# Moving steps between stages of a two-block transformer kernel: gate order, state stages, a fence, and the head of the recurrence

## The chip, the cores and the metric

The kernel runs on one core of a Trainium2 chip, as one program with an instruction stream for each engine: TensorE (PE) for matrix products, VectorE (DVE), ScalarE (ACT) and GpSimd (POOL) for the rest, and SyncE (SP), which issues most DMA transfers. ACT issues some transfers too, from its own stream. Every engine runs its instructions in program order and waits on semaphores for the others. The metric is the device time of one execution in microseconds, lower is better; the time of a version is the median of its runs.

## The reference

Two blocks follow each other on a sequence of 512 rows of width 1024, all in fp32. The first has three branches on an input normed and modulated by a condition: a state-space scan in four groups and both directions, a windowed attention that also looks at a context of 256 rows, and gates that merge them; then a feed-forward with a convolution. Cut to what the change touches:

```python
mod = jax.nn.silu(c) @ w_mod[l] + b_mod[l]                      # also for the context
h_lat = modulate(x, norm1_g[l], sh1, sc1)                       # rmsnorm(x, g) * (1 + sc1) + sh1
p_lat = h_lat @ w_in                                            # z, xbc, dt, q, k, v, gates
xbc = jax.nn.silu(dwconv_centred(xbc_raw, conv_w, conv_b))
states = jnp.einsum('bcsgn,bgrcs,bcsgrp->bcgrpn', bc, decay_to_end, xc)   # per chunk of 128
att_lat = window_ctx_attention(q_l, k_l, v_l, k_c, v_c, sink)
out = (g_ssd * (y_ssd @ w_o_ssd) + g_att * (y_att @ w_o_att)) @ w_out
```

The second block has a forgetting attention, a complex diagonal recurrence (s5) and an attention on a memory:

```python
log_f = jax.nn.log_sigmoid(fl + b_forget)                       # softplus, 12 heads
F = jnp.cumsum(log_f, axis=1)                                   # added to the scores of y_fox
ab = exp(lam * step); bb = (ab - 1) / lam * b                   # numbers of the recurrence, complex
x_re = jnp.einsum('gph,blgh->blgp', bb_re, u)
h = associative_scan(ab, x)                                     # along the 512 rows
y = Re(c h) + d * u
```

## The kernel before

**Products.** A product in fp32 is made as three products of halves: every operand is split into a high part (a cast to fp32r) and a low part (the rest), and PE adds high x high, low x high and high x low (L792 to L794, or L849 to L851 with the roles changed). So a projection of 128 output columns for 512 rows takes 24 matmuls of 128x512 over the eight parts of its input. Weights arrive in blocks of 512 KB. SP issues them (L2658) in a fixed order into four slots of raw weights (`raww`, RAWS = 4). ACT casts the high part (`whi`, L1243), POOL subtracts for the low part (`wlo`, L2486). A slot is free for the block four places later when its subtraction is done; a block of `w_mod` isn't split, PE reads it raw (L928), and its slot is free after that. ACT's casts stand in its stream among its other work, two split blocks ahead of PE (AHEAD = 2). What else ACT does at that place has to wait until the block has landed.

**Order.** `order()` writes one list of steps, and every engine runs its share of each step in that order. Lists of two tasks are merged by `merge()`, which takes the next step from the task that is behind by the costs in SHARE; `alternate()` takes them in turn. The steps that matter here:

- `mod j n`: a quarter of modulation row j, PE L928. `modt` and `modsel` (L936) bring a row into columns, `modout` writes shift `modS` and, for the scale, `A1` (L1933).
- `rms in`: the inverse root of the mean squares, spread over the partitions in PSUM by PE (L831). `xnorm j` multiplies `xin` by it (L1921). `h1 j` makes hv = xin·A1 + modS (DVE L1945 and L1946, for j = 1, 4, 7 on ACT), its high part `hT_h` on ACT (L1262) and its low part `hT_l` on DVE (L1707) for even j, POOL (L2502) for odd j. `dtx` multiplies two parts of h by the first weights, dt and one xbc block, which `bring` loads and splits.
- `dt 0` to `dt 5`: softplus of dt, its running sums, their transposes `csT`, which ACT writes to DRAM (`csd`, L1338 and L1342) for later loads of `ec`. `taps g m`: a convolution of B or C (`BTs`, ACT L1271, DVE L1755 and L1758).
- `state g d n`: in each of four groups, ten steps of xw = xtok·wdec on DVE (L1803), its product with B on PE (L1018) and the update of the state. They are merged in groups 1 to 3 with four projections `z` (gated by ACT and DVE into `yg`, ACT L1396 to L1404) and eight quarters of modulation rows. The `ssd_chunks` behind them are merged with the next group's xbc projections.
- `fence att`, `reload`, `qpair k`: the attention's output qT becomes the pair `qp_h`, `qp_l` for the projection `oa`; reload brings `yp` back from DRAM (L1478). The 16 projections `gate` stand beside the window attention.
- In the second block: `u` (the s5 input), `fl` and `forget` (PE L808, DVE L2367, softplus L1763 to L1776 with ACT L1266 and L1268, scan L2374), `s5num` (the numbers of the recurrence, in `pk`, DVE L1823, ACT L1534 to L1538), `s5bar`, 22 steps `s5pow` of powers, `fq`/`tm` (q, k and v of the attention), and `fscore`, `fpt`, `fpv` (scores L1182, row maximum L1781, exponential `Pf` L1278).

## Time and profile before

| | us |
|---|---|
| median of 3 runs | 2195.9 |
| lowest and highest run | 2193.11 and 2197.08 |
| the profiled execution | 2190.85 |
| its span | 2188.4 |

| engine | busy us | share of the span |
|---|---|---|
| PE (matmuls) | 2031.3 | 93% |
| DVE | 1068.3 | 49% |
| ACT | 863.1 | 39% |
| POOL | 815.3 | 37% |

The span is the time between the first and the last instruction of the profiled execution; what lies around it is 2.45 us. The trace is read as timelines: the instructions of an engine with their start, their duration and, in brackets, the time for which the engine stood idle before and what ended that. "x2" at the end of a row means that two instructions that follow each other are one row. Rows of ACTq and SPq are the time in which an engine's queue issues transfers, not the transfer. The granted clock is the share of full speed that PE was given.

### The profile page before, as it was taken

How to read it: one execution, taken by the hardware profiler on the slowest of the kernel's cores; microseconds unless marked ns; L12 is line 12 of the kernel's file. 1: busy time of each engine (PE TensorE's matmuls, PEld its weight loads, DVE VectorE, ACT ScalarE, POOL GpSimd, SP SyncE). 2: the span in 40 equal slices, each digit the busy share in tenths (PEclk: the TensorE clock that was granted, in tenths of full speed). 3: DMA queues.
4: the chain of work that ended last, by engine and by line, in shares of the span. 5: the costliest groups of instructions: out<-in, count | busy, mean ns of one | idle time of the engine just before them, and what ended most of it. 6: DMA issues, size and time to landing. Idle time of an engine off the chain costs nothing.

```text
span 2188.4 us, 28557 instructions
## 1 busy us (share of the span) xinstructions
PE 2031.3 (93%) x11586; PEld 1648.7 (75%) x11586; DVE 1068.3 (49%) x1741; ACT 863.1 (39%) x1563; POOL 815.3 (37%) x455
## 2 busy tenths in 40 slices
PE   4879898999999999999899999988898988999997
PEld 3758686878877787888778888876677766788886
DVE  4469685858455545531444441137544565611112
ACT  2435353535344444323343443233544443532221
POOL 1302121212343323466443444442532461544442
PEclk8999999999999999999999999989999999999998
DMA  7234545354211114323244333334112323243331
GB/s 261 68 110 155 183 144 195 134 177 160 87 58 39 49 41 162 116 95 109 87 135 135 97 94 96 99 108 135 58 58 63 86 55 86 81 134 97 96 106 58
DMA packets 89251, 235.63 MB, mean 108 GB/s; under 512 B 27424, under 2 KB 30624, under 8 KB 88224
## 3 DMA queue, kind: packets, MB, share of 16 engines
q1 hardware_dynamic: 85712, 225.16, 31.8%
q10 hardware_dynamic: 3408, 8.65, 1.0%
q8 instruction: 91, 1.49, 0.3%
q14 instruction: 40, 0.33, 0.0%
HBM read 220.51 MB, written 12.19 MB: 106 GB/s over the span
## 4 chain that ended last, share of the span: by engine, by line
PE 80%; DVE 12%; ACT 4%; issue 1%; DMA 1%; POOL 1%; SPq 0%; ACTq 0%; DVEq 0%; POOLq 0%
PE ps L792 21%; PE ps L794 20%; PE ps L793 20%; PE ps L1123 1%; PE ps L1018 1%; PE ps L1110 1%; PE ps L1182 1%; PE ps L1098 1%; PE ps L928 1%; PE ps L1040 1%; DVE ec L2052 1%; PE ps L1038 1%; PE ps L1039 1%; DVE xw L1803 1%; PE ps L1099 1%
## 5 line engine op out<-in xcount | busy, mean ns | idle before, releaser
L2486 POOL TENSOR_TENSOR wlo<-raww,whi 128x1024 fp32r<-128x1024 f32 (+2 forms) x253 | 590.0, 2338 | 949.5 <-ACT whi L1243 945.2
L1243 ACT CAST whi<-raww 128x1024 fp32r<-128x1024 f32 (+2 forms) x284 | 285.1, 1007 | 251.5 <-PE ps L794 183.8
L792 PE MATMUL ps<-hT_h,whi 128*128 128x512 f32 (+1 forms) x688 | 260.6, 379 | 7.4 <-DVE BTs L1758 6.8
L794 PE MATMUL ps<-hT_h,wlo 128*128 128x512 f32 (+1 forms) x688 | 251.9, 366 | 0.0
L793 PE MATMUL ps<-hT_l,whi 128*128 128x512 f32 (+1 forms) x688 | 251.8, 366 | 0.0
L792 PE MATMUL ps<-H_h,whi 128*128 128x512 f32 x480 | 190.6, 397 | 9.7 <-ACT qk L1554 4.1
L793 PE MATMUL ps<-H_l,whi 128*128 128x512 f32 x480 | 187.3, 390 | 0.0
L794 PE MATMUL ps<-H_h,wlo 128*128 128x512 f32 x480 | 187.1, 390 | 0.0
L792 PEld LDWEIGHTS ps<-hT_h,whi 128*128 128x128 f32 x688 | 131.1, 191 | 32.7 <-DVE BTs L1758 7.1
L1796 DVE SCALAR_TENSOR_TENSOR gt<-gt,ps 128x512 f32<-128x512 f32 x40 | 27.5, 688 | 250.8 <-PE ps L794 250.8
L793 PEld LDWEIGHTS ps<-hT_l,whi 128*128 128x128 f32 x688 | 131.0, 190 | 22.5 <-issue 2.6
L794 PEld LDWEIGHTS ps<-hT_h,wlo 128*128 128x128 f32 x688 | 130.5, 190 | 21.2
L792 PE MATMUL ps<-h_h,whi 128*128 128x512 f32 x336 | 132.2, 393 | 0.8 <-ACT mk L1526 0.8
L793 PE MATMUL ps<-h_l,whi 128*128 128x512 f32 x336 | 131.1, 390 | 0.0
L794 PE MATMUL ps<-h_h,wlo 128*128 128x512 f32 x336 | 130.9, 389 | 0.0
L792 PEld LDWEIGHTS ps<-H_h,whi 128*128 128x128 f32 x480 | 90.5, 189 | 33.4 <-ACT qk L1554 5.5
L794 PEld LDWEIGHTS ps<-H_h,wlo 128*128 128x128 f32 x480 | 90.2, 188 | 19.2
L793 PEld LDWEIGHTS ps<-H_l,whi 128*128 128x128 f32 x480 | 90.3, 188 | 18.6 <-issue 0.5
L1389 ACT ACTIVATE ec<-ec,la 128x128 f32<-128x128 f32 x256 | 77.3, 389 | 52.9 <-DVE ec L2052 52.9
L1755 DVE SCALAR_TENSOR_TENSOR ua<-ps,vc,ua 128x511 f32<-128x511 f32 x44 | 33.0, 750 | 109.7 <-ACT ua L1271 109.7
L1781 DVE TENSOR_REDUCE small<-ps 128x1 f32<-128x513 f32 (+1 forms) x64 | 48.3, 755 | 72.5 <-PE ps L1103 52.9
L792 PEld LDWEIGHTS ps<-h_h,whi 128*128 128x128 f32 x336 | 63.1, 188 | 15.8 <-issue 1.6
(521 smaller groups left out, 4676.1 us busy)
## 6 DMA issues: line engine op xcount, KB each, us to landing
ec<-csd SPq DMA_DIRECT2D x32, 1024.0 KB, 7.8
raww<-in_w_mod SPq DMA_DIRECT2D x48, 512.0 KB, 4.7
raww<-in_w_up SPq DMA_DIRECT2D x44, 512.0 KB, 3.7
raww<-in_w_xbc SPq DMA_DIRECT2D x24, 512.0 KB, 4.5
raww<-in_w_gl SPq DMA_DIRECT2D x24, 512.0 KB, 3.4
raww<-in_w_z SPq DMA_DIRECT2D x16, 512.0 KB, 4.8
raww<-in_w_g SPq DMA_DIRECT2D x16, 512.0 KB, 3.4
raww<-in_w_os SPq DMA_DIRECT2D x16, 512.0 KB, 3.7
```

Source lines behind the costliest of these rows:

```text
L792: e.matmul(o, whi[:, i, c], hi(k)[:, t0:t1], start=(k == 0), stop=False)
L793: e.matmul(o, whi[:, i, c], lo(k)[:, t0:t1], start=False, stop=False)
L794: last = e.matmul(o, wlo[:, i, c], hi(k)[:, t0:t1], start=False, stop=(k == kt - 1))
L928: last = e.matmul(ps[32 * q:32 * q + 32, b, 0:128], cs_[:, 4 * n + 2 * kk:4 * n + 2 * kk + 32], raww[:, p % RAWS, kk * 512 + q * 128:kk * ...
L1018: e.matmul(ps[:, b, :], Btok[:, CHUNKS[d][n], :], xw[:, i, :], start=True, stop=True).then_inc(*ssd_done.mark(("state", g, d, n), ("free", ...
L1038: e.matmul(o, xtok[:, c, h], inner(g, c, 0)[:, r, :], start=True, stop=False)
L1243: e.copy(o, x.rearrange("p (k c) -> p k c", c=64) if p == plan.first["dt", 0] else x).then_inc(*w_high.mark(("high", p)))
L1389: last = e.activation(E[:, r, :], E[:, r, :], ACT.Exp, bias=la[:, c, h:h + 1])
L1755: e.scalar_tensor_tensor(out=dst[:, 1:T], in0=psum[:, 0:T - 1], scalar=V(names[0], m), in1=dst[:, 1:T], op0=ALU.mult, op1=ALU.add).then_in ...
L1781: e.tensor_reduce(sm[:, 1:2], S, AXX, ALU.max, negate=True).then_inc(*v_step.mark(event))
L1796: e.scalar_tensor_tensor(out=x, in0=x, scalar=1.0, in1=psum, op0=ALU.add, op1=ALU.mult).then_inc(*v_moved.mark(*events))
L2486: e.tensor_tensor(o, x, h.bitcast(F32), ALU.subtract).then_inc(*p_wlow.mark(("split", p), ("raw free", p)))
```

## The change

- **Start.** `bring` goes ahead of all of `w_mod`. `xnorm` is gone: DVE makes hv = xin·A1·(spread root) from PSUM in one scalar_tensor_tensor for each of the two widths (512 and 256), ACT adds the shift while it writes the high part, and DVE makes the low part, (hv + modS) - hT_h, in two pieces, for all eight rows. POOL has no part in it any more. The spread root lies in PSUM until the last row is made, so that the ring of banks for `rms in` is one shorter. `dtx 0` stands behind the last quarter of row 3.
- **SHARE.** New costs. They move `taps(0,4)` ahead of `dt 5`, and small steps elsewhere.
- **State stages 1 to 3.** `z_mod_steps` writes the order of z projections and modulation quarters by hand, in place of `alternate`.
- **Fence att.** PE doesn't wait there for the other engines; `gate 15` stands behind the fence, ahead of the pairs; `reload` comes after `gateout 15` and waits for that projection.
- **Second block.** `fl` and `forget` stand ahead of `u 4`, `u 5`, the first `fq` and `s5num`. Of the 22 `s5pow` steps 16 stood ahead of the first `fscore` and 6 behind it; now 6 stand ahead and 16 behind.

```diff
-SHARE = {"dt": 2.4, "x1": 1.2, "state0": 10.56, "xbc0": 5.76, "xbc1": 13.1, "taps0": 0.05, "taps1": 0.01,
+SHARE = {"dt": 2.4, "x1": 1.92, "state0": 6.34, "xbc0": 5.18, "xbc1": 13.1, "taps0": 0.36, "taps1": 0.01,
...
+def z_mod_steps(g, j, k):
+
+    z, m = z_steps(g), lambda j: [(SHARE["mod"], [("mod", j, n)]) for n in range(4)]
+    a, b, t = m(j), m(k), lambda j: [(0.1, [("modt", j)])]
+    sel = lambda j: [(0.1, [("modsel", j)]), (0.0, [("modout", j)])]
+    return (z[:1] + a[:2] + z[1:3] + a[2:] + t(j) + z[3:6] + sel(j) + b[:2] + z[6:9] + b[2:] + t(k) + z[9:11] + sel(k) + z[11:])
...
-    return out + sum((gate_steps(i) for i in range(11, 16)), [])
+    return out + sum((gate_steps(i) for i in range(11, 15)), [])
...
-    o = [("init",), ("norm1",)] + a[0] + a[1] + a[2] + [("total", "in")] + a[3] + [("modt", 0)]
...
-    o += c[3] + [("modt", 1), ("h1", 2), ("xnorm", 4), ("bring",), ("h1", 3), ("xnorm", 5)]
-    o += d[0] + [("modsel", 1), ("modout", 1)] + d[1] + [("xnorm", 6), ("dtx", 0)] + d[2] + [("xnorm", 7)] + d[3] + [("modt", 3), ("dtx", 1)]
-    o += [("modsel", 3), ("modout", 3), ("h1", 4), ("h1", 5), ("dtx", 2), ("h1", 6), ("h1", 7), ("dtx", 3)]
+    o = [("init",), ("norm1",), ("bring",)] + a[0] + a[1] + a[2] + [("total", "in")] + a[3] + [("modt", 0)]
...
+    o += d[0] + [("modsel", 1), ("modout", 1)] + d[1] + [("h1", 3)] + d[2] + d[3] + [("modt", 3), ("dtx", 0), ("modsel", 3), ("modout", 3)]
+    o += [("h1", 4), ("dtx", 1), ("h1", 5), ("h1", 6), ("dtx", 2), ("h1", 7), ("dtx", 3)]
...
-    o += merge(ssd_states(1), alternate(z_steps(0), mod_steps((4, 5)))) + merge(ssd_chunks(1), xbc_steps(2))
...
+    o += merge(ssd_states(1), z_mod_steps(0, 4, 5)) + merge(ssd_chunks(1), xbc_steps(2))
...
-    o += [("fence", "att"), ("reload",)] + [("qpair", k) for k in range(8)]
+    o += [("fence", "att"), ("gate", 15)] + [("qpair", k) for k in range(8)] + [("gateout", 15), ("reload",)]
...
-    o += [("fence", "two"), ("s5load",), ("s5num",), ("u", 4), ("u", 5)] + [("s5u", m) for m in range(3)]
-    chain = [(SHARE["fl"], [("fl",)]), (SHARE["forget"], [("forget",)]), (SHARE["fq"], [("fq", 0)]), (SHARE["fq"], [("fqout", 0), ("fq", 6)]), (0.0, [("fqout", 6)])]
+    o += [("fence", "two"), ("fl",), ("s5load",), ("forget",), ("u", 4), ("u", 5), ("fq", 0), ("s5num",)] + [("s5u", m) for m in range(3)]
+    chain = [(SHARE["fq"], [("fqout", 0), ("fq", 6)]), (0.0, [("fqout", 6)])]
...
                     elif s[1] == "att":
                         fence(PE, "att")
-                        others(PE, "att")
...
+                    ACTE.wait_ge(at("h", j))
+                    ACTE.wait_ge(at("mod", j))
+                    v = hv[:, j % 4, :]
+                    e.activation(hT_h[:, j, 0:L], v[:, 0:L], ACT.Identity, bias=modS[:, j, 0:1]).then_inc(*x_high.mark(("high part", "hT", j)))
+                    e.activation(hT_h[:, j, L:LT], v[:, L:LT], ACT.Identity, bias=modS[:, j, 1:2]).then_inc(*x_high.mark(("high part", "hT", j)))
...
+            def shifted_low1(j):
+                DVE.wait_ge(at("high part", "hT", j))
+                DVE.wait_ge(at("mod", j))
+                for q, (t0, t1) in enumerate(ALL):
+                    last = e.scalar_tensor_tensor(out=hT_l[:, j, t0:t1], in0=hv[:, j % 4, t0:t1], scalar=modS[:, j, q:q + 1],
+                                                  in1=hT_h[:, j, t0:t1].bitcast(F32), op0=ALU.add, op1=ALU.subtract)
...
+                    for q, (t0, t1) in enumerate(ALL):
+                        last = e.scalar_tensor_tensor(out=v[:, t0:t1], in0=xin[:, j, t0:t1], scalar=A1[:, j, q:q + 1], in1=r[:, t0:t1], op0=ALU.mult, op1=ALU.mult)
...
+                    if j:
+                        shifted_low1(j - 1)
```

How the order shows on the engines, at three places. First ACT around dt 5, before and after; `csd` is DRAM, `BTs_78` the B of group 0, `wdec` and `csT` come from dt's sums:

```order
53 L1334 ACTIVATE wdec<-wdec 128x384
54 L1243 CAST whi<-raww 128x1024
55 L1338 DMA csd<-csT 2x32x128 x4
56 L1339 ACTIVATE ecsT<-csT 64x512
57 L1342 DMA csd<-ecsT 2x32x128 x4
58 L1271 ACTIVATE BTs_78<-ps,vc 128x512
59 L1271 ACTIVATE BTs_78<-ps,vc 128x256
```

```order
56 L1327 ACTIVATE wdec<-wdec 128x384
57 L1240 CAST whi<-raww 128x1024
58 L1268 ACTIVATE BTs_78<-ps,vc 128x512
59 L1268 ACTIVATE BTs_78<-ps,vc 128x256
60 L1331 DMA csd<-csT 2x32x128 x4
61 L1332 ACTIVATE ecsT<-csT 64x512
62 L1335 DMA csd<-ecsT 2x32x128 x4
63 L1357 ACTIVATE sq<-BTs_78 128x512
```

The two activations into BTs_78 now stand ahead of the eight issues into csd.

Second, the end of state stage 1 on PE, before and after, from the last products of the last z projection (L794, in the new file L792) to the step that turns the modulation row. The raw modulation blocks are `raww`, the state products `xw,Btok`:

```order
830 L794 MATMUL ps<-hT_h,wlo 128x512
831 L928 MATMUL ps<-raww,cs__56 32x128 x8
832 L1018 MATMUL ps<-xw,Btok 128x512
833 L928 MATMUL ps<-raww,cs__56 32x128 x8
834 L1018 MATMUL ps<-xw,Btok 128x512
835 L928 MATMUL ps<-raww,cs__56 32x128 x8
836 L1018 MATMUL ps<-xw,Btok 128x512
837 L928 MATMUL ps<-raww,cs__56 32x128 x8
838 L1018 MATMUL ps<-xw,Btok 128x512
839 L936 MATMUL ps<-cst,mrow 128x8
```

```order
830 L792 MATMUL ps<-hT_h,wlo 128x512
831 L926 MATMUL ps<-raww,cs__56 32x128 x8
832 L1016 MATMUL ps<-xw,Btok 128x512
833 L926 MATMUL ps<-raww,cs__56 32x128 x8
834 L1016 MATMUL ps<-xw,Btok 128x512
835 L934 MATMUL ps<-cst,mrow 128x8
```

Behind the last z projection stood four modulation blocks, each with a state product; now two do, and the other two stand ahead of its 24 matmuls.

Third, the head of the recurrence on DVE, before and after. `ffs` are the forget gates, `FT` their sums, `apow` and `pk` the recurrence's powers and numbers, `X` the residual rows:

```order
1003 L1823 TENSOR_TENSOR apow<-apow,vtmp 128x24x2
1004 L1763 SCALAR_TENSOR_TENSOR ffs<-ffs 12x512
1005 L1765 TENSOR_SCALAR ffs<-ffs 12x512
1006 L1767 SCALAR_TENSOR_TENSOR ffs<-ffs 12x512
1007 L1770 RECIPROCAL ffs<-ffs 12x512
1008 L1772 SCALAR_TENSOR_TENSOR ffs<-ffs 12x512
1009 L1774 TENSOR_TENSOR ffs<-ffs 12x512
1010 L1776 SCALAR_TENSOR_TENSOR ffs<-ffs 12x512
1011 L2374 SCALAR_TENSOR_TENSOR FT<-cst,ffs 12x512
```

```order
975 L2236 SCALAR_TENSOR_TENSOR X<-X,vc,ps 128x512 x8
976 L2367 TENSOR_SCALAR ffs<-ps,vc 12x512
977 L1767 SCALAR_TENSOR_TENSOR ffs<-ffs 12x512
978 L1769 TENSOR_SCALAR ffs<-ffs 12x512
979 L1771 SCALAR_TENSOR_TENSOR ffs<-ffs 12x512
980 L1774 RECIPROCAL ffs<-ffs 12x512
981 L1776 SCALAR_TENSOR_TENSOR ffs<-ffs 12x512
982 L1778 TENSOR_TENSOR ffs<-ffs 12x512
983 L1780 SCALAR_TENSOR_TENSOR ffs<-ffs 12x512
984 L2374 SCALAR_TENSOR_TENSOR FT<-cst,ffs 12x512
985 L2249 MEMSET Tp 128x1024
986 L1827 TENSOR_TENSOR pk__63<-vc,pk__63 128x24 x2
```

The gates' softplus and scan stood behind the numbers and the first powers; now they follow the last rows of X, and the numbers come behind them.

## Rows read from the trace of the kernel before

**Rows 1.** The page, part 1: busy us (share of the span) xinstructions.

```profile
PE 2031.3 (93%) x11586; PEld 1648.7 (75%) x11586; DVE 1068.3 (49%) x1741; ACT 863.1 (39%) x1563; POOL 815.3 (37%) x455
```

**Rows 2.** Windows: us, busy us (instructions) by engine, granted clock, DMA share, GB/s.

```profile
250.00:275.00 25.00, 19.50 (x128) 13.48 (x127) 22.63 (x29) 11.39 (x26) 5.05 (x3) 0.86 0.50 162
...
845.00:870.00 25.00, 20.08 (x111) 15.47 (x111) 14.93 (x17) 11.46 (x20) 11.63 (x7) 0.86 0.68 269
1490.00:1550.00 60.00, 46.24 (x234) 36.71 (x232) 49.52 (x143) 20.85 (x38) 18.00 (x8) 0.86 0.28 86
```

**Rows 3.** Timeline of PE at the start: start, us, engine, line, operation [idle <-releaser].

```profile
40.60 1.08 PE L928 MATMUL ps<-raww,cs__56 128*32 128x128 f32 x16 [4.20 <-DMA raww<-in_w_mod]
...
47.16 0.80 PE L959 MATMUL ps<-hT_h,whi 128*128 128x512 f32 x1 [3.94 <-DVE xin L1921]
...
61.13 0.79 PE L959 MATMUL ps<-hT_h,whi 128*128 128x512 f32 x1 [3.73 <-DVE hT_l L1707]
```

**Rows 4.** Timeline of SP at the start; then source L2186 (ns min/median/max).

```profile
31.80 0.40 SPq L2658 DMA_DIRECT2D raww<-in_w_dt  x1
...
L2186 DVE SCALAR_TENSOR_TENSOR vt<-X,A,ps x8: 742/748/748, 1060.8 to 1078.2; 128x512 f32<-128x512 f32 x8
```

**Rows 5.** Timelines of ACT and its queue, then PE, at dt 5.

```profile
117.09 2.68 ACTq L1338 DMA_DIRECT2D csd<-csT  x4
...
122.63 1.23 ACT L1271 ACTIVATE BTs<-ps,vc 128x512 f32<-128x512 f32 x2 [2.19 <-issue]
...
125.03 0.80 PE L792 MATMUL ps<-hT_h,whi 128*128 128x512 f32 x1 [6.83 <-DVE BTs L1758]
```

**Rows 6.** Timelines in state stage 1: PE, SP, ACT, DVE, POOL; last, tile xw's DVE line.

```profile
256.57 1.12 PE L1018 MATMUL ps<-xw,Btok 128*128 128x512 f32 x2
...
263.77 2.05 PE L1018 MATMUL ps<-xw,Btok 128*128 128x512 f32 x2 [5.50 <-DVE xw L1803]
...
253.44 9.99 SPq L2658 DMA_DIRECT2D raww<-in_w_xbc  x6
...
256.84 1.05 ACT L1243 CAST whi<-raww 128x1024 fp32r<-128x1024 f32 x1 [6.45 <-DMA raww<-in_w_xbc]
...
260.79 2.83 DVE L1803 TENSOR_TENSOR xw<-xtok,wdec 128x512 f32<-128x512 f32 x1
...
260.68 2.40 POOL L2486 TENSOR_TENSOR wlo<-raww,whi 128x1024 fp32r<-128x1024 f32 x1 [0.36 <-ACT whi L1243]
...
L1803 DVE TENSOR_TENSOR xw<-xtok,wdec x40: 680/685/2839, 130.0 to 493.6; 128x512 f32<-128x512 f32 x40
```

**Rows 7.** Timelines at the fence "att": ACT and its queue, then PE.

```profile
853.75 1.91 ACTq L1478 DMA_DIRECT2D yp_l<-ysc  x4
855.69 4.26 ACT L1262 CAST qp_h<-qT 128x512 fp32r<-128x512 f32 x8 [4.44 <-issue]
...
857.89 0.77 PE L792 MATMUL ps<-qp_h,whi 128*128 128x512 f32 x1 [4.92 <-ACT qp_h L1262]
...
861.44 0.63 PE L794 MATMUL ps<-qp_h,wlo 128*128 128x512 f32 x1
...
864.10 0.39 PE L793 MATMUL ps<-qp_l,whi 128*128 128x512 f32 x1
864.33 0.39 PE L794 MATMUL ps<-qp_h,wlo 128*128 128x512 f32 x1
```

**Rows 8.** Timelines at the start of the s5 stage: ACT, DVE, then PE.

```profile
1504.66 0.63 ACT L1266 ACTIVATE ffs<-ffs 12x512 f32<-12x512 f32 x1 [14.22 <-DVE ffs L1763]
...
1516.97 1.21 DVE L2374 TENSOR_TENSOR_SCAN FT<-cst,ffs 12x512 f32<-12x512 f32 x1
...
1513.04 0.55 PE L849 MATMUL ps<-whi,H_h 128*128 128x256 f32 x1 [6.91 <-POOL wlo L2486]
...
1539.04 1.65 PE L1182 MATMUL ps<-qk 128*128 128x384 f32 x2 [4.32 <-ACT Pf L1278]
...
1549.97 0.91 PE L1182 MATMUL ps<-qk 128*128 128x384 f32 x2 [0.24 <-ACT Pf L1278]
```

More of the change, by code:

```diff
@@ L1053, in tensor_program @@
                     if n == "in":
[L1054 removed]
+                        spread(("rms", n), 3, LT, (5,), at("root", n))
                     elif n == "x2":
@@ L1476, in scalar_program @@
                 elif k == "reload":
+                    ACTE.wait_ge(at("gemm", ("gate", 15), 0))
                     for i in range(4):
@@ L1725, in shifted_low @@
                                        op0=ALU.add, op1=ALU.subtract).then_inc(*v_xlow.mark(("pair", "h2", j), ("free", "vt2", j)))
+            def shifted_low1(j):
[4 more added lines that the diff above has]
+                                                  in1=hT_h[:, j, t0:t1].bitcast(F32), op0=ALU.add, op1=ALU.subtract)
+                    if q == 0:
+                        last.then_inc(*v_xlow.mark(("pair", "hT", j)))
+                last.then_inc(*v_xlow.mark(("pair", "hT", j), ("free", "hv", j)))
             def rms(n):
```

72 lines of the change are left out of this document (22 added, 50 removed).

## The prediction

> **What bounds the kernel now.** I read the page's list of busy times first: TensorE (PE) is busy for 93% of the span, 2031.3 us, and the other engines for half or less [rows 1]. So about 157 us is all that a new order can win in idle time, beside what the clock gives back. The second view is the table of stretches, where a reader should see that PE's idle time isn't even. In three short stretches PE is busy for 19.50 of 25, 20.08 of 25 and 46.24 of 60 us, and the granted clock is 0.86 there [rows 2]. The third view is the timeline of PE with what ended each idle time, and then the same stretch on the engine named. Each hole is followed by slow work: the pair of state products that takes 1.12 us ahead of the hole that ends at 263.77 takes 2.05 us after it [rows 6], the ratio of the 2.4 to the 1.2 GHz level. A hole costs its idle time, and some 2 to 3 us of slower products behind it.
>
> **The change part by part.** All terms are made against the profiled execution, 2190.85 us (span 2188.4); the median of the runs, 2195.9, is 5.05 above it, and I carry the difference over. No arithmetic of weight on PE is added or removed: the change moves steps in all five engines' programs.
>
> *Start (h1).* PE waits 4.20 us for a block of w_mod, 3.94 for `xin` from VectorE (DVE) and 3.73 for `hT_l` [rows 3]. Removed are eight products of 128x768 on DVE, the two-step tensor_scalar of five of the rows there and that of three on ScalarE (ACT), and the low parts of four rows on GpSimd (POOL). Added, for each of the eight rows, are a product from PSUM of 512 columns, which takes 0.748 in the norm of the second half of the block [rows 4], one of 256 (estimate 0.45), and the low part in two pieces (0.7 and 0.45, from the same width). That is some 2.4 us for each row on DVE, 19 in all, which is no less than what goes. It isn't a gain in itself. What gains is the order. The weights of dt and the first xbc block are now loaded ahead of w_mod, not at 31.80 behind twelve of its blocks [rows 4], and dtx 0 stands behind the last mod rather than amid them. Against it, w_mod's third and later blocks wait until ACT and POOL have split the two blocks in front, which I put at 4.6 us from casts and subtractions that take 1.05 and 2.40 each elsewhere [rows 6], partly beside each other. Of 3.94 + 3.73 + 4.20 = 11.9 us of waits and some 3 us of clock, less 4.6 and less about 5 us in which DVE paces the last four rows (4 x 2.4, half of it beside PE's work), there remain 5.5 us. The bounds are 0 (DVE paces all) and 9.
>
> *dt 5 and the taps.* PE stands still for 6.83 us until `BTs` are there. ACT had not come to them: it issued four transfers of csd from 117.09 for 2.68 us and four more after that, and began with BTs at 122.63 [rows 5]. The issues alone hold ACT back by 5.5 us. In the new order taps(0,4) stands ahead of dt 5, so BTs starts at about 117 and the issues run while DVE and PE work. The price is the delay of csd, whose reader, the load of ec, isn't due before the chunks. Gain: the 6.83, less some 3 that ACT and DVE need for BTs in any order (from 122.63 to 125.03 and a little more), plus 2 of clock, is 6; bounds 3 and 9.
>
> *State stages 1 to 3.* In stage 1 PE finishes the last mod block at about 258.3 and waits 5.50 us for `xw`; the two later stages have the same hole (one of three is shown). Followed back: DVE's xw takes 2.83 us beside a subtraction of 2.40 on POOL, against a median of 0.685 over 40; DVE had itself waited for ACT's sq, and ACT had waited 6.45 us for the first block of w_xbc, which SyncE (SP) could issue only at 253.44, when PE had freed a slot of raw weights [rows 6]. In the old order four mod blocks stand behind the last z product; in the new one two stand ahead of it and two behind, so the slot of the first xbc block comes free before z's 24 products of 0.23 us from start to start [rows 7], 5.5 us earlier. ACT's cast then lies behind PE's work, its sq is not late, and xw is not late either. Each hole is worth 5.5 plus 2.6 of clock. I take 6 (18 for three), since ACT, DVE and POOL still have the same work in the same few microseconds. Bounds: 10 and 24.
>
> Here the Trainium skill bears on the row, in "SBUF — State Buffer", section "SBUF: two separate sides": VectorE with two operands in SBUF and GpSimd reading SBUF hold a shared pair of ports as "an exclusive lock, not a bandwidth split". The 2.83 beside POOL's 2.40 agrees. By this rule the hole would shrink only as far as POOL's subtraction moves off xw: if it still meets xw, 2.1 us remain in each stage and the three give 12, not 18.
>
> *The fence "att".* PE waits 4.92 us until `qp_h` is there, because ACT issues four transfers (1.91 us) before its casts and PE has nothing in between [rows 7]. Now one projection of 24 products (gate 15, 5.5 us) stands there, and the transfers are issued after it. It covers the wait whole; with the 15 or so products behind it that took 0.63 rather than 0.39 each (3 us, since they overlap) the hole is worth 7.9. Left over is what gate 15 lost where it stood, as cover for the last window softmax. Gain 6.5; bounds 3 and 7.5.
>
> *Start of the recurrence (s5).* The forget gates end with a scan at 1516.97. ACT had waited 14.22 us for DVE with their first exponential, and all its casts of weights stood behind that. PE therefore waited 6.91 us at 1513.04 for wlo, and 4.32 at 1539.04 for `Pf`, where the row maximum stood behind DVE's power steps [rows 8]. The stretch lacks 60 - 46.24 = 13.8 us of PE and 14% of its clock [rows 2]. In the new order forget stands ahead of the numbers and the first power steps, so its scan ends at least those 14.22 us earlier, by 1504, and ACT's wait lies where DVE has nothing else to do and is short. Idle 13.8 and clock 4 are the most there is. I take 11: both waits (11.2), plus 3 of clock, less 3 for ten more power steps (16 rather than 6) among the scores. There they cost little so far: PE's wait at 1549.97, with a step on either side, is 0.24 [rows 8]. Bounds 5 and 17.
>
> *The rest.* Small moves in the window stage and the late s5 steps touch small waits like that 0.24 each: 0, bounds -5 and +5.
>
> **The sum** is 5.5 + 6 + 18 + 6.5 + 11 + 0 = 47 us: 2190.85 - 47 = 2143.9 profiled, 2195.9 - 47 = 2149 on the runs' scale.
>
> **Rivals.** *Holes move on* (a half gain). The xbc block comes earlier, but one resource later is as late: z's own block must now be loaded and split behind two mod blocks, and POOL's subtraction meets xw. The state stages then give 9, and in the s5 stage ACT's wait moves from softplus to the numbers' three activations, which gives 6 less; the start gives 0. Sum 9 less, 6 less and 5.5 less: 26, or 2170. For it speak the 2.83 of xw; against it, that ACT's wait of 6.45 names a transfer, not POOL.
>
> *All holes close* with the clock: each bound's upper part, 5.5 + 8 + 23 + 7.5 + 15 = 59, or 2137. It needs DVE off the path everywhere.
>
> *The power steps land on the scores* (slower). Sixteen steps stand among scores whose row maximum queues behind them on DVE. If each is stretched by POOL as xw is, by 2.1 us, and its own length, an estimate of 1.4 us from the steps' small operations, is exposed as well, that is 16 x 3.5 = 56, less the 47: 9 us slower, 2205. It decides from 47 / 16 = 2.9 us exposed for each step. The wait of 0.24 beside such a step speaks against it.
>
> *Nothing gained*: the waits swap places and the times stay, 2196. It would need every term at its low bound and the last at its worst (0 + 3 + 10 + 3 + 5 - 5 = 16, still faster), so it is unlikely.
>
> **How the numbers follow.** The forecast, 2141 to 2160, has a chance of 0.50; all holes closing 0.15; holes moving on 0.27; nothing gained 0.03; slower 0.05. Faster by over 0.2% (4.4 us, about what a measurement of this kernel can tell from no change) is 0.92, within it 0.03, slower 0.05. The range runs from the sum of all upper bounds, 9 + 9 + 24 + 7.5 + 17 = 66.5, which is 2129, and 1 for the runs' spread, to 2170 and 6 more for the last term's bound and the same spread: 2128 to 2176.
>
> **What would show it.** Right: no PE wait above 2 us behind the last mod block in the three state stages; ACT's BTs ahead of csd and PE's wait there under 2 us; gate 15 between the last window product and the first with qp_h, and no wait; the scan ended by 1504 and the second score block of the forgetting attention reached 10 us earlier than 1539; no PE wait of over 3 us between dtx 1 and dtx 3. Wrong: a PE wait on a z product's `wlo` in a state stage, xw at 2.8 again with PE waiting, ACT idle behind `pk` with casts queued, or PE waiting for Pf by over 1 us in several places of 1525 to 1590.

## The result and the profile after

The changed kernel takes 2174.36 us (median of 4 runs, 2171.24 to 2177.91) against 2195.87 before (2193.11 to 2197.08): the ratio is 0.9904, with a 95% interval of 0.9885 to 0.9923. It is 21.5 us faster where 47 were forecast. The profiled execution after took 2175.76 us (span 2174.4), against 2190.85 before; it gained 15.1 us, less than the medians, since it lies 1.4 us above the median of its kernel and that of before 5.0 below. Of the runs below one (stages 2 and 3 undone) took 4804.77 us, where the four others of its kernel took 2171 to 2180, and is left out of its median.

The page's first part after, to be read beside [rows 1]: PE's instructions are as many, and what changed is above all its idle time. The span is 14.0 us shorter; 11.2 of that are idle time, and 2.8 are products that ran faster (mean granted clock 0.979, before 0.973).

```profile
PE 2028.5 (93%) x11586; PEld 1648.7 (76%) x11586; DVE 1075.7 (49%) x1749; ACT 863.2 (40%) x1565; POOL 813.3 (37%) x453
```

The windows after that hold the work of [rows 2] (us, busy us and instructions by engine, granted clock, DMA share, GB/s), and with them those of stages 2 and 3:

```profile
245.00:270.00 25.00, 24.43 (x162) 19.94 (x162) 23.24 (x29) 13.73 (x31) 9.06 (x4) 1.00 0.45 146
345.00:370.00 25.00, 21.20 (x134) 14.59 (x133) 20.17 (x28) 9.48 (x15) 7.45 (x3) 0.93 0.53 180
480.00:505.00 25.00, 20.04 (x173) 19.69 (x172) 20.77 (x25) 13.05 (x39) 2.45 (x1) 0.86 0.48 165
```

Stage 1 is full at full clock (24.43 of 25 us; 19.50 before). Stage 3's window isn't: there the hole is still 5 us and the clock 0.86.

**Where the time went.** Steps have moved, so a row of before has no row of after at its place. I therefore added up PE's rows of each trace in order of time, a product of n columns counted as n/512 x 0.2275 us (what one takes from start to start at full clock), and compared the times at which both kernels had the same amount of work behind them. I call this the ledger. The unit is such a microsecond of work; "gain" is how much further ahead the changed kernel got in that stretch. The fence's hole lies at 658.5, so the window stage is counted to 655.

| stretch (work done, us) | forecast | gain after |
|---|---|---|
| start, to the first dt products (0 to 40) | 5.5 | 1.4 |
| dt 5, taps and group 0 (40 to 160) | 6 | 8.2 |
| state stage 1 (160 to 200) | 6 | 6.3 |
| state stage 2 (200 to 300) | 6 | 0.9 |
| state stage 3 and its chunks (300 to 440) | 6 | -0.7 |
| window stage (440 to 655) | 0 | -8.8 |
| the fence "att" (655 to 680) | 6.5 | 7.0 |
| to the second block's last u (680 to 1260) | 0 | -0.4 |
| head of the recurrence (1260 to 1300) | 11 (whole stage) | 12.1 |
| the rest of that stage (1300 to 1520) | | -12.2 |
| to the end | 0 | 0.2 |
| sum | 47 | 14.0 |

One execution isn't the kernel. At the same order of steps, stage 1 gained 5.1 to 6.8 us in 16 traces (mean 5.9), stage 2 gained 0.9 to 5.2 in 15 (mean 3.0), and stage 3 with its chunks -2.2 to -0.6 in eight (mean -1.3). So the 0.9 of stage 2 in this trace is at the low end.

Three terms came as forecast (dt 5, stage 1, the fence, whose 6.5 was meant less what gate 15 costs the window stage), one was too large (the start), two gained next to nothing here (stages 2 and 3), the window stage lost what the fence won and more, and the head's gain was given back entirely. PE's rows with idle time say by what. Timeline of PE after:

```profile
364.32 1.33 PE L1016 MATMUL ps<-xw,Btok 128*128 128x512 f32 x2 [3.10 <-DVE xw L1807]
...
489.38 0.66 PE L1036 MATMUL ps<-ec,xtok 128*64 128x128 f32 x2 [4.96 <-DVE ec L2064]
...
605.91 0.33 PE L1107 MATMUL ps<-cst,Pm 128*128 128x128 f32 x1 [1.96 <-DVE Pm L1795]
...
729.71 0.65 PE L1120 MATMUL ps<-PT,vt 128*64 128x256 f32 x4 [2.24 <-DVE PT L2147]
...
845.16 0.47 PE L790 MATMUL ps<-qp_h,whi 128*128 128x512 f32 x1 [0.59 <-POOL qp_l L2502]
...
1559.09 1.65 PE L1179 MATMUL ps<-qk 128*128 128x384 f32 x2 [5.44 <-ACT Pf L1275]
...
1821.39 1.19 PE L1161 MATMUL ps<-Hp,Qc 128*128 128x128 f32 x4 [6.18 <-DMA Tp<-kd]
```

The 4.92 of [rows 7] is 0.59 at 845.16, the 6.91 of [rows 8] is 1.73 (at 1492.36), and the 6.83 of [rows 5] is gone. New are 4.96 us at 489.38 (for ec, in stage 3's first chunk; 1.11 before), 5.44 for Pf at 1559.09 and 6.18 for a transfer at 1821.39.

**Stage 1 against stage 2**, whose steps stand in the same order. Timelines of ACT, DVE and PE after; first stage 1, then stage 2:

```profile
242.93 1.05 ACT L1240 CAST whi<-raww 128x1024 fp32r<-128x1024 f32 x1 [6.29 <-DMA raww<-in_w_xbc]
...
247.55 2.85 DVE L1807 TENSOR_TENSOR xw<-xtok,wdec 128x512 f32<-128x512 f32 x1
...
250.54 1.10 PE L1016 MATMUL ps<-xw,Btok 128*128 128x512 f32 x2 [0.57 <-DVE xw L1807]
...
356.76 1.05 ACT L1240 CAST whi<-raww 128x1024 fp32r<-128x1024 f32 x1 [9.14 <-DMA raww<-in_w_xbc]
...
361.34 2.83 DVE L1807 TENSOR_TENSOR xw<-xtok,wdec 128x512 f32<-128x512 f32 x1
```

and the queue that issues the blocks, SP, in the same two places:

```profile
238.55 0.80 SPq L2654 DMA_DIRECT2D raww<-in_w_xbc  x2
...
350.73 9.24 SPq L2654 DMA_DIRECT2D raww<-in_w_xbc  x3
```

The block is 4.4 us under way in stage 1 (238.55 to 242.93) and 6.0 in stage 2 (350.73 to 356.76). From the issue to the end of xw it is 11.9 us and 13.4 us, and PE's cover (z's 24 products, two mod blocks, a state product) is some 11. So the hole is 0.57 in one and 3.10 in the other. Of the 2.5 us between them the landing makes 1.6; the other 0.9 is cover: PE reached the product 11.4 us after the issue in stage 1 and 10.5 in stage 2. Neither is a property of the stage. At this order the same block was under way for 3.8 to 5.6 us in stage 1 (16 traces) and for 3.8 to 6.0 in stage 2 (15), and the hole at the end of stage 2 was anything from under 0.5 us (three traces) to 3.1. In both, xw takes 2.85 and 2.83 us as before [rows 6]: POOL's subtraction still stands beside it.

### The profile page after: what moved, and what is told of

Read it like the earlier page. It is cut to its first block, busy times and chain, and to the rows that moved or that the text cites. A ratio compares the mean times of both kernels' runs of the same rounds, so it can differ in the third digit from the quotient of the medians.

```text
span 2174.4 us, 28587 instructions
## 1 busy us (share of the span) xinstructions
PE 2028.5 (93%) x11586; PEld 1648.7 (76%) x11586; DVE 1075.7 (49%) x1749; ACT 863.2 (40%) x1565; POOL 813.3 (37%) x453
## 3 DMA queue, kind: packets, MB, share of 16 engines
q1 hardware_dynamic: 85712, 225.16, 31.9%
## 4 chain that ended last, share of the span: by engine, by line
PE 80%; DVE 11%; ACT 4%; DMA 2%; issue 2%; POOL 1%; SPq 0%; ACTq 0%; DVEq 0%; POOLq 0%
PE ps L790 20%; PE ps L791 20%; PE ps L792 20%; PE ps L1107 1%; PE ps L1120 1%; PE ps L1095 1%; PE ps L1038 1%; PE ps L926 1%; PE ps L1179 1%; PE ps L1036 1%; PE ps L1016 1%; PE ps L1037 1%; PE ps L1039 1%; DVE xw L1807 1%; PE ps L1161 1%
## 5 line engine op out<-in xcount | busy, mean ns | idle before, releaser
L2486 POOL TENSOR_TENSOR wlo<-raww,whi 128x1024 fp32r<-128x1024 f32 (+3 forms) x255 | 596.5, 2345 | 980.3 <-ACT whi L1240 976.0
L792 PE MATMUL ps<-hT_h,wlo 128*128 128x512 f32 (+1 forms) x688 | 250.7, 364 | 0.0
L792 PE MATMUL ps<-H_h,wlo 128*128 128x512 f32 x480 | 187.0, 390 | 0.0
L792 PEld LDWEIGHTS ps<-hT_h,wlo 128*128 128x128 f32 x688 | 129.9, 189 | 21.0
L792 PE MATMUL ps<-h_h,wlo 128*128 128x512 f32 x336 | 130.8, 389 | 0.0
L792 PEld LDWEIGHTS ps<-H_h,wlo 128*128 128x128 f32 x480 | 90.1, 188 | 19.0
L1275 ACT ACTIVATE Pm<-ps,small 128x513 f32<-128x513 f32 (+1 forms) x64 | 47.6, 744 | 82.7 <-DVE small L1785 82.4
```

Source lines behind the costliest of these rows:

```text
L792: last = e.matmul(o, wlo[:, i, c], hi(k)[:, t0:t1], start=False, stop=(k == kt - 1))
L1275: e.activation(dst, S, ACT.Exp, bias=sm[:, 1:2], accum_out=sm[:, 2:3]).then_inc(*a_func.mark(event, drained))
L2486: e.tensor_tensor(o, x, h.bitcast(F32), ALU.subtract).then_inc(*p_wlow.mark(("split", p), ("raw free", p)))
```

## The experiments

The runs are given as medians, each beside the kernel before on the same chip, with the ratio and its interval. An interval is about 0.15 to 0.2% wide to each side, 3 to 4 us; so I also give the ledger of PE's work by stretch. In most stretches it repeats better: the window stage lost 8.6 to 9.9 us in six of the seven traces with the new order there and gate 15 behind the fence, and 5.4 in the seventh. A difference of 2 or 3 us that one trace shows in one stretch isn't shown by it alone.

**The window stage: order or missing gate?** Its loss of 8.8 us has two candidates in the diff: the new places of `q`, `qrot` and `gate`, or gate 15, which no longer covers the last rows.

```diff
-"score": 4.99, "pt": 1.4, "pv": 1.61, "q": 8.33, "qrot": 3.05, "kst": 0.84
+"score": 1.66, "pt": 1.12, "pv": 0.82, "q": 7.57, "qrot": 2.5, "kst": 0.0
-    return out + sum((gate_steps(i) for i in range(11, 15)), [])
+    return out + sum((gate_steps(i) for i in range(11, 15)), []) + [(SHARE["gate"], [])]
```

> The changed kernel, with the order of the window stage as before (without gate 15, which stays behind the fence). In the changed kernel PE does the work between the start of the window stage and the fence 9 us slower than before, by the work done against time. Theory: the new places of q, qrot and gate among scores cost this (PE waits for DVE's Pm and PT); then the window stage gets back 5 to 9 us, and the run is 5 to 9 us below the changed kernel (2166 to 2169). Rival: the loss is gate 15, which covered the last softmax rows and is missing there; then nothing comes back from the order and the run is within 2 us of the changed kernel (2174).

Measured: 2169.62 us, ratio 0.9885 (0.987 to 0.99). The window stage lost 2.0 us instead of 8.8, with gate 15 behind the fence as in the changed kernel, and the waits for Pm and PT there are those of before (1.05, 0.94 and 1.03 us). The seven later kernels with this order lost 2.0 to 2.1 us. The medians, 4.7 us apart, point the same way, but their intervals overlap.

```diff
-    return out + sum((gate_steps(i) for i in range(11, 15)), [])
+    return out + sum((gate_steps(i) for i in range(11, 16)), [])
-    o += [("fence", "att"), ("gate", 15)] + [("qpair", k) for k in range(8)] + [("gateout", 15), ("reload",)]
+    o += [("fence", "att"), ("reload",)] + [("qpair", k) for k in range(8)]
+                        others(PE, "att")
-                    ACTE.wait_ge(at("gemm", ("gate", 15), 0))
```

> The changed kernel, with the part at the fence undone: gate 15 among the window's steps, the reload ahead of the pairs, and PE's wait for all engines. Theory (order of q, qrot, gate is at fault in the window): the fence's 6.6 us hole comes back, the window loses as much as in the changed kernel, so 5 to 7 us slower than the changed kernel (2180). Rival (gate 15 is missed in the window): the window gets back what the fence loses, within 2 us of the changed kernel.

Measured: 2177.51, ratio 0.9926 (0.9908 to 0.9944), 3 us slower than the changed kernel, which the runs alone don't separate. By the ledger the stretch from 440 to 700 loses 5.6 us against 1.8 in the changed kernel: the fence's part is worth 3.8. With the window order of before that stretch gains 5.0, in all eight traces: 7.0 at the fence, less 2.0 for the cover that gate 15 gave in the window stage. So of the 8.8 us the order is at fault for 6.8 and the missing gate for 2.0: the new costs moved 5.5 us projections from ahead of DVE's row maxima to other places, where Pm and PT are waited for. (With the new order and the gate in its old place the window stage lost 5.5, not 8.8. Since one trace without the gate lost as little, a larger share of the gate at that order is neither shown nor excluded.)

**The second block: are the powers at fault for what is given back?** Both runs put the 22 power steps of the recurrence early again, by an empty step ahead of the other chain, the second with all costs of that block as before, which is exactly the order of before from the first q pair on.

```diff
-    chain = [(SHARE["fq"], [("fqout", 0), ("fq", 6)]), (0.0, [("fqout", 6)])]
+    chain = [(SHARE["fl"] + SHARE["forget"] + SHARE["fq"], []), (SHARE["fq"], [("fqout", 0), ("fq", 6)]), (0.0, [("fqout", 6)])]
```

> The changed kernel, with the 22 power steps of the recurrence placed early again, as far as an empty step ahead of the second chain does it (8 of them before the values of the attention, 16 before its first score), with the new costs otherwise. PE reaches the first score 23 us earlier than before and has given back 10 to 13 of that by 1830 us. Theory: the powers among the scores cost it (PE waits 5.44 us for Pf at 1559, beside power steps of DVE that take 1.0 us in place of 0.26); then 5 to 10 us come back (2164 to 2169). Rival: the gift is lost later anyway, since the recurrence's chain on DVE, POOL and DMA is the bound of that stage and only starts as early as its numbers allow; then within 2 us of the changed kernel.

> As the run with the powers early, and with the costs of all steps of the second block as before, which gives exactly the order of before from the first q pair on. If the new costs of the late s5 steps are at fault (the wait of 6.18 us for Tp from DRAM at 1821), this is 3 to 6 us faster than the run with the powers early alone; if the order isn't the reason, both are alike and as slow as the changed kernel.

Measured: 2208.34, ratio 1.006 (1.0041 to 1.0079), and 2175.75, ratio 0.9915 (0.9897 to 0.9933). Both theories fell for the first: it was 34 us slower than the changed kernel. The second is as fast as the changed kernel, 33 us faster than the first, where the theory had 3 to 6. They have 15 and 16 of the 22 powers ahead of the scores and differ in the costs alone. In both, PE's first wait for Pf is longer than it ever was (13.13 and 13.08 us), so this wait isn't what makes one of them slow; the ledger of 1300 to 1520 loses 33.8 us in the first and 3.4 in the second. Timeline of PE, powers early:

```profile
1524.04 1.65 PE L1179 MATMUL ps<-qk 128*128 128x384 f32 x2 [13.13 <-ACT Pf L1275]
```

**Three places outside the block** that the trace offered, with the window order of before: modulation row 3 is turned ahead of dtx 0, and in chunk 0 of group 3 another product of v covers ec.

```diff
-... + d[3] + [("modt", 3), ("dtx", 0), ("modsel", 3), ("modout", 3)]
+... + d[3] + [("modt", 3), ("modsel", 3), ("modout", 3), ("dtx", 0)]
+    late = [("tmout", "w_v", 0, 1), ("tm", "w_v", 0, 2)]
+    o = [s for s in o if s not in late]
+    i = o.index(("out", 3, 0))
+    o[i:i] = late
```

> The changed kernel with three edits in three stretches that don't touch: the window stage's order as before (as in the first run of this study); at the start the step that turns modulation row 3 ahead of dtx 0; in chunk 0 of group 3 the third product of v (tm, 2.9 us of PE) ahead of the outputs that wait for DVE's ec. Theory at the start: A1 of the last four rows waits on PE's order alone (the turn ran at 55.18 us, behind dtx 0), so DVE begins h1 4 some 6 us earlier and PE's waits of 2.10 and 1.58 go: 3 us. Theory in group 3: DVE's chain (xw, gating, ec) is what is late, and 2.9 of the 4.96 us can be covered: 3 us. Rival at the start: the load of the next blocks is late; at group 3: PE's extra step only moves the wait to the next chunk; then 0 each. Theory 2162 to 2165, rivals 2169.

Measured: 2162.06, ratio 0.9851 (0.9836 to 0.9866), as the theories had it. By the ledger the start gained 7.9 us against before (the four kernels with this start 5.8 to 7.9, mean 6.9; the nine without it -0.2 to 4.5, mean 2.5), and stage 3 with its chunks 3.9 instead of -0.7 (the seven kernels with this edit mean 3.1, the eight without it -1.3). PE's wait for ec (timeline of PE, three places) is 1.19, where it was 4.96:

```profile
480.78 0.40 PE L1033 MATMUL ps<-ec,xtok 128*64 128x128 f32 x2 [1.19 <-DVE ec L2061]
```

The turn that ran at 55.18 behind dtx 0 runs at 48.18, and the waits of 2.10 and 1.58 us between the dtx products are gone.

**POOL beside the powers.** In the changed kernel DVE and POOL meet where PE waits 5.44 us. Timelines of DVE, then POOL, after:

```profile
1550.00 1.00 DVE L1827 TENSOR_TENSOR q<-q,pk__63 128x96 f32<-128x96 f32 x1
1551.03 1.00 DVE L1827 TENSOR_TENSOR q<-q,vtmp 128x96 f32<-128x96 f32 x1
...
1549.81 1.08 POOL L2567 TENSOR_TENSOR BA<-bbar,arev 128x512 f32<-128x512 f32 x1
1550.85 1.07 POOL L2568 TENSOR_TENSOR ptmp<-bbar,arev 128x512 f32<-128x512 f32 x1
```

Each of these two operations of DVE lasts about as long as POOL's beside it; operations of the same shape took 0.26 us at 1546.74 and 1547.04, with POOL idle.

```diff
                     POOL.wait_ge(at("factor powers"))
+                    POOL.wait_ge(at("phase powers"))
```

> The changed kernel; POOL starts the first table of the recurrence only when DVE has made the last power (one wait more). In the changed kernel DVE's operations on q and pk took 1.00 and 2.47 us instead of 0.26 and 0.62 while POOL made that table at 1549.8 to 1556.9. Theory (POOL's collisions with the powers cause PE's wait of 5.44 us for Pf): that wait falls to 2 us or less and the run is 2 to 4 us faster. Rival (the time is set by the recurrence's chain, which now starts its table 7 us later): same or 1 to 3 us slower.

Measured: 2174.71, ratio 0.9913 (0.9901 to 0.9926). PE's wait at that place fell to 1.76 us, and the ledger, counted from the block's start, was 3.5 us better at 1340; at 1520 it was level. The collision is real and cost that wait; it isn't what the stage's end waits for. Timeline of PE, POOL behind the powers, at that wait:

```profile
1552.69 0.91 PE L1179 MATMUL ps<-qk 128*128 128x384 f32 x2 [1.76 <-ACT Pf L1275]
```

**Stages 2 and 3, and the second block, undone.** The first puts these two stages in exactly the order of before (the costs of before are set while they are merged; the chunks behind stage 3 keep their new places), the second the whole second block.

```diff
-    o += merge(ssd_states(2), z_mod_steps(1, 6, 7)) + merge(ssd_chunks(2), xbc_steps(3))
-    o += merge(ssd_states(3), z_mod_steps(2, 8, 9)) + merge(ssd_chunks(3), kv_steps())
+    o += with_costs_of_before(lambda: merge(ssd_states(2), alternate(z_steps(1), mod_steps((6, 7))))) + merge(ssd_chunks(2), xbc_steps(3))
+    o += with_costs_of_before(lambda: merge(ssd_states(3), alternate(z_steps(2), mod_steps((8, 9))))) + merge(ssd_chunks(3), kv_steps())
```

> The changed kernel, with state stages 2 and 3 in exactly the order of before; stage 1 keeps the new order. By the traces stage 1 gained 6 us and stages 2 and 3 together less than 1. Theory (DVE's work is the bound there, the holes moved inside the stage and into the first chunk): within 1.5 us of the changed kernel (2173 to 2176). Rival (the new order does gain in stages 2 and 3, and something else lost it): 6 to 12 us slower.

```diff
-    o += [("fence", "two"), ("fl",), ("s5load",), ("forget",), ("u", 4), ("u", 5), ("fq", 0), ("s5num",)] + [("s5u", m) for m in range(3)]
-    chain = [(SHARE["fq"], [("fqout", 0), ("fq", 6)]), (0.0, [("fqout", 6)])]
+    o += [("fence", "two"), ("s5load",), ("s5num",), ("u", 4), ("u", 5)] + [("s5u", m) for m in range(3)]
+    chain = [(SHARE["fl"], [("fl",)]), (SHARE["forget"], [("forget",)]), (SHARE["fq"], [("fq", 0)]), (SHARE["fq"], [("fqout", 0), ("fq", 6)]), (0.0, [("fqout", 6)])]
```

> The changed kernel, with the second block in exactly the order of before (gates behind the numbers, all costs of that block as before). PE reached the first scores 12.7 us earlier by the work done in the changed kernel and was no more ahead at 1860 us than at the block's start. Theory (the new order of that stage gains nothing in the end): within 2 us of the changed kernel. Rival (the forecast's: the head's gain is real and another thing lost it by chance in that trace): 8 to 12 us slower, 2182 to 2186.

Measured: 2175.53 (median of the four that count), ratio 0.9912 (0.9897 to 0.9927), and 2176.21, ratio 0.9919 (0.9905 to 0.9932). Neither differs from the changed kernel beyond the intervals. With the order of before, stage 2 gained 0.3 by the ledger (mean 3.0 with the new one) and stage 3 with its chunks 0.0 (-1.3): by these the new order of both is worth 1 to 2 us, and the medians, 1.2 us apart, don't speak against it. The new order of the second block is worth nothing measurable as a whole.

**What decides in the second block?** Four kernels on the one with three places (2162.06): costs of before with the new head; the same with 12 rather than 7 powers ahead of the scores; part of the powers' arithmetic left out; and the blocks brought later.

```diff
-"fv": 2.7, "fscore": 0.45, "fpv": 3.9, "s5bar": 3.3, "s5x": 4.0, "s5scan": 2.19, "s5tab": 8.71, "s5g": 4.62, "s5out": 6.33, "s5k": 1.02
+"fv": 3.0, "fscore": 0.36, "fpv": 3.12, "s5bar": 3.0, "s5x": 5.0, "s5scan": 2.43, "s5tab": 8.22, "s5g": 5.76, "s5out": 4.0, "s5k": 1.44
```

> The kernel with the three edits (2162), with all costs of the second block as before: the first score still has only 7 of 22 power steps ahead of it, the later steps of the recurrence stand up to one head later. Theory A (the total of DVE's work decides, the order of the late steps does little): within 3 us of 2162. Theory B (the new costs of the late steps are at fault for the 7 us lost between 1650 and 1720): 4 to 8 us faster.

```diff
+    chain = [(9.3, []), (SHARE["fq"], [("fqout", 0), ("fq", 6)]), (0.0, [("fqout", 6)])]
```

> As the run with the costs of before, with an empty step of half the cost ahead of the second chain: 12 of 22 power steps ahead of the first score. Theory A: each power step costs PE as much ahead of the scores as among them, so within 3 us of the run with 7 ahead. Rival: there is a place between where they lie beside PE's work; then 5 us or more faster than both.

```diff
-                        cmul((part(tab, 0, k, 2 * k), part(tab, 1, k, 2 * k)), (part(tab, 0, 0, k), part(tab, 1, 0, k)), (K(12), K(13)), k,
-                             vtmp[:, 0:24 * k].rearrange("p (a b) -> p a b", b=k))
+                        for q in (0, 1):
+                            tt(part(tab, q, k, 2 * k), part(tab, q, 0, k), K(12).unsqueeze(2).to_broadcast([P, 24, k]), ALU.mult)
```

> The kernel with the three edits (2162), leaving out part of the arithmetic of the powers: each of the six doublings of the tables z8 and q8 is two products instead of six operations on DVE, so that the recurrence's numbers are not the reference's. It takes 24 operations of 0.2 to 0.26 us plus their gaps, some 6 us, off DVE between 1500 and 1560 us. Theory (DVE's work decides the stretch up to the first scores and what is paid among them): 4 to 7 us faster, about 2157. Rival (another chain, of POOL or of transfers, decides at the end): the ledger of that stretch shows the gain and loses it by 1860 us, within 2 us of 2162.

```diff
-    o = [("init",), ("norm1",), ("bring",)] + a[0] + a[1] + a[2] + [("total", "in")] + a[3] + [("modt", 0)]
+    o = [("init",), ("norm1",)] + a[0] + a[1] + a[2] + [("total", "in")] + a[3] + [("modt", 0), ("bring",)]
```

> The kernel with the three edits (2162), with the blocks of dt and xbc brought after the fourth block of w_mod instead of ahead of the first. In the changed kernel the total of squares ran at 23.37 us (18.70 before), since PE stood in front of a w_mod block that came late, and all of h1 with it. Theory: the root is back at 27 us, the first row of h 5 us earlier, dtx 0 up to 4 us earlier: 2158 to 2160. Rival (PE's modulation blocks end late by the transfers whatever their order, at 49 us): within 1 us of 2162.

Measured: 2188.75 (0.9979, 0.9968 to 0.9989), 2186.23 (0.9963, 0.9948 to 0.9978), 2156.32 (0.9834, 0.9818 to 0.985) and 2158.8 (0.9845, 0.9829 to 0.9861). The first is 27 us slower, which neither theory had: A fell outright, and B had the wrong sign. The ledger loses 29 us between 1400 and 1520; PE's waits there are for Pq (11.9 us in all), Pf (7.4) and PTm (4.5). That the costs of before, with the powers late, put the late steps of the recurrence behind too much of the attention, where no projection is left to lay beside them, fits this, but isn't shown. Twelve power steps ahead don't help (second). Taking some 6 us of work off DVE gives 5.7 (third); the intervals of the two kernels just overlap, and the ledger of the block has 4.9. The medians don't tell the fourth from the kernel with three places, but by the ledger the start gains 2 to 3 us more with the blocks behind the fourth block of w_mod (8.5 to 10.8 in three kernels, mean 9.4, against 6.9).

In the ledger from 1260 to the end, the combinations stand like this: new costs with 6 powers ahead of the scores 1.0 to -4.4 (six traces), with 15 ahead -32.7 (two traces); costs of before with 7 ahead -31.9, with 12 ahead -26.7, with 16 ahead -2.4 and -2.0.

**The end of the stage, and the head alone.** The first two are edits on the fastest, 2158.8; the third is the changed kernel with the old head.

```diff
     o += merge(s5_steps(), chain)
+    o.remove(("gm", 3))
+    o.insert(o.index(("s5out", 5)), ("gm", 3))
```

> The fastest kernel so far (2158.8: three edits and bring later), with the projection gm 3 (5.5 us of PE) ahead of the recurrence's last output step instead of behind it. PE waited 6.05 us there for Tp, which comes back from DRAM. Theory (part of the head's gain is lost at this wait, since the other chain has nothing left to lay beside it): 3 to 5 us faster, 2154 to 2156. Rival (the projection was cover for the gelu behind that step, and its wait appears there): within 1.5 us of 2158.8.

```diff
                     POOL.wait_ge(at("factor powers"))
+                    POOL.wait_ge(at("phase powers"))
```

> As the run before, and POOL's first table waits for the last power. By the ledger of PE's work this wait alone saved 3 us at 1600 us and nothing at the stage's end. Theory (the stage's end was bound by the transfer then): now 2 to 3 us faster than the run before. Rival (the table comes late for the first g step in any case): same or slower.

> The changed kernel (2174) with the steps at the head of the recurrence in the order of before (numbers, then fl and forget) and all new costs kept. Theory A (DVE's work ahead of the scores is the bound, so the head's order is worth 2 us at most and the costs only fit themselves to it): 2174 to 2178. Theory B (head and costs belong together, as the slow run with the old costs says): 10 us slower or more, 2185.

Measured: 2162.33 (0.9865, 0.9849 to 0.9882), 2159.44 (0.984, 0.9827 to 0.9855) and 2206.53 (1.0057, 1.0044 to 1.0069). The wait for Tp is gone with gm 3 ahead of it, but nothing is gained: PE now waits 4.94 us there, at 1799.05, for a sq of DVE, as the rival had it. POOL's wait on top of that is 2.9 us faster by the medians, inside the intervals, and 0.5 by the ledger of the block.

The third run settles the head. Its steps from the first fq 6 on stand in exactly the order of the run with the powers early; only the head differs, and both take the same: 2206.53 and 2208.34. Their ledgers are 9 us apart at 1280 (the scan is early in one) and within 0.4 us of each other from 1300 to the end. The same holds with the order of before behind the head: 2175.75 with the new head, 2176.21 with the old, and -2.4 and -2.0 by the block's ledger. So at a fixed order of what follows, the head is worth nothing that the medians (2 us apart at most) or the ledgers (0.4 us) show, twice. Timelines of DVE: powers early, whose first row begins the forget gates and whose second is their scan:

```profile
1468.27 0.74 DVE L2367 TENSOR_SCALAR ffs<-ps,vc 12x512 f32<-12x512 f32 x1 [14.33 <-PE ps L808]
...
1480.10 1.21 DVE L2374 TENSOR_TENSOR_SCAN FT<-cst,ffs 12x512 f32<-12x512 f32 x1
```

and the head undone, numbers first:

```profile
1467.27 0.91 DVE L2249 MEMSET Tp<- 128x1024 f32 x1 [13.23 <-DMA xsc<-X]
...
1502.29 1.21 DVE L2374 TENSOR_TENSOR_SCAN FT<-cst,ffs 12x512 f32<-12x512 f32 x1
```

Timeline of PE, head undone, the first wait for Pf:

```profile
1524.30 1.65 PE L1179 MATMUL ps<-qk 128*128 128x384 f32 x2 [4.03 <-ACT Pf L1275]
```

The scan comes 22 us earlier with the new head, and the score behind it starts at the same time, 1524.04 against 1524.30. DVE idles 14.33 us ahead of the block in one case (until fl is projected) and 13.23 in the other (until X is in DRAM); then it has the same work ahead of the first row maxima in both.

## Why the prediction was wrong

The direction was right, the size was not: 21.5 us against 47, in the range of 2128 to 2176 at its upper end and under half of the forecast gain. (The range's lower end leaves out the upper bound of 5 of the last term; with it the range would begin at 2123.) Of the signs that it named, those of being wrong came at three places: PE waited 3.10 us for xw at the end of stage 2 with xw at 2.83 us, and for Pf 1.07 us at 1535.80 and 5.44 at 1559.09. Step by step:

- **Start, 5.5: a term too large.** 1.4 us in the changed kernel's trace and 2.5 on average. The 4.6 us for blocks behind dt's was right in kind (PE waited 2.90 us at 22.36 and the sum of squares ran at 23.37, not 18.70). What I missed is that the turn of row 3, two small products of 0.29 us together, was put behind dtx 0 in PE's order, and with it A1 of the last four rows; the wait of 2.10 us at 58.71 is for that. Moving it gave 4 us.
- **dt 5, 6: right**, 8.2 us with all of the stretch up to group 0. Where the 2 us more come from isn't shown.
- **State stages, 18: 6.5 came** (7.6 by the means over the traces). The first stage was right in mechanism and size. In the other two the step "each hole is worth 5.5 plus 2.6 of clock, I take 6" took a chain of 12 to 13 us against a cover of 11 as covered. The same order leaves 0.57 us where the block lands in 4.4 us and 3.10 where it takes 6.0 and the cover is 0.9 us shorter, and in the other traces under 0.5 to 3.1 at the end of stage 2; what remained went in waits of 0.7 to 0.9 us for xw earlier in the stage. In stage 3 the hole moved to the first chunk: DVE works without a gap from xw to ec, and PE waits 4.96 us for ec with only two half-size products between. That is the rival "holes move on", with ec the late one and not z's block. The Trainium skill's rule on the shared ports ("SBUF — State Buffer", "SBUF: two separate sides") had it that xw stays long as long as POOL's subtraction meets it. The trace agrees: 2.85 and 2.83 us in the changed kernel, and by that rule I had 12 rather than 18.
- **The fence, 6.5: right in kind, too large by 1.5 to 3.** At the hole it gained 7.0 us (of the 7.9), but gate 15 took 2.0 from the window stage, not 1.4: the net is 5.0 at the window order of before, and 3.8 by undoing it at the new one, both inside its bounds of 3 and 7.5.
- **"The rest", 0 with bounds -5 and +5: wrong**, -8.8 in the window stage. I had read the window stage's edits as small moves of equal worth. The order of before in that stage gives 6.8 us back; this was the largest single error that an experiment repaired.
- **The recurrence, 11: wrong.** Both waits were measured rightly, and both went (6.91 to 1.73, 4.32 to 1.98). The step that failed is that their removal was a gain: "ACT's wait lies where DVE has nothing else to do and is short". DVE's idle time ahead of the block was not used by the new head (13.25 us before, 14.32 after, since fl is projected as late as X is written), so DVE's work ahead of and among the first scores is unchanged, and PE pays for it there or later. The ledger has it: 12.1 us won at the head, 12.2 lost behind it. The rival of the power steps named the place and the row maximum; its price (16 x 3.5) was too high, but the 5.44 us at 1559 are it, and 3.7 of them come from POOL's table beside the powers. What the stage gives back after 1600 is not settled as a single cause: it takes the arithmetic on DVE (some 5 of 6 us came through), while 24 to 34 us are at stake in how the costs and the place of the powers go together. It isn't the head that the new costs need: with the new head and the powers early they are 34 us slower, with the old head (powers early too) 32. They go with the powers late, and the costs of before with the powers early; the costs of before with the powers late are 27 us slower. Why a mismatch costs so much stays open.

The table's terms add up to 14.0 us, the difference of the two spans. The runs' medians say 21.5, give or take 4; most of the 7.5 between is the place of the two profiled executions among their runs (5.05 us below the median, and 1.4 above).

**A faster kernel than both.** The changed kernel with the window order of before, row 3's turn ahead of dtx 0, one more product of v ahead of the outputs of chunk 0, and dt's and xbc's blocks brought behind w_mod's fourth: 2158.8 us, ratio to before 0.9845 (0.9829 to 0.9861). It is 15.6 us faster than the changed kernel by the medians (13 by the ratios, since the two were measured beside different runs of the kernel before) and 35 faster than before. Every edit in it is an order of steps.

## What to carry to other kernels

A wait that a trace shows need not be a gain when it goes: at the head two waits of PE went and the time stayed. Ask whether the move fills a gap on that engine, or merely exchanges two pieces of its work. Count the whole chain behind a transfer (landing, cast, subtraction, the vector work beside it) against the cover in microseconds; with less than 1 us to spare, equal stages come out differently, and so does one stage from run to run. And when a table of costs orders several stages, look at each stage's new order as a change of its own: here one stage's new costs lost 7 us without anyone's intent, and another's were worth 30 us in combination and nothing in sum. One trace of a kernel gives a stretch only within what its runs differ by: stage 2's gain was 0.9 us in the first trace and 3.0 in the mean of 15.

## What the runs showed of the hardware

- One 512 KB block of weights, at the same place of the same order, took from 3.8 to 5.6 us from issue to landing in 16 traces of stage 1, and from 3.8 to 6.0 in 15 traces of stage 2; in the changed kernel's trace it was 4.4 and 6.0.
- A DVE operation with two operands in SBUF lasted as long as POOL's operation beside it: 1.00 us instead of 0.26 for 128x96, beside POOL operations of 1.07 and 1.08. Letting POOL wait took 3.7 us from one wait of PE.
- Two kernels whose orders agree from one step on came within 0.4 us of each other's ledger over the 600 us that followed, though they began 9 us apart. State stage 2 didn't repeat so well: at one order its gain spread over 4.3 us.
